# An attention pipeline one step deeper, with its PSUM banks divided by kind of product

## The chip, the cores and the metric

One NeuronCore of a Trainium2 chip runs the whole program. The metric is the device time of one execution in microseconds (us). Lower is better.

## The reference

Two transformer blocks, one after the other, on 256 image tokens and 256 context tokens of width 1024, all in float32. The first has three branches (a pooling mixer, a differential attention, a recurrent RWKV scan in both directions), a gated merge and a mixture of 32 experts. The second has two layers: an even one with a low-rank attention and a neighbourhood attention, and an odd one with a sliding-window attention with sinks, each followed by a gated feed-forward part. The change touches only the three attentions. All three compute, for blocks of 128 queries and for two heads (or two maps of one head) at a time:

```
s = q @ k.T * scale (+ bias)
p = softmax(s)                     # with a sink in the denominator in the odd layer
a = p[:, :, 0] - lam * p[:, :, 1]  # only in the differential attention
out = a @ v
```

## The kernel before

TensorE (PE in the profile), ScalarE (ACT), VectorE (DVE) and the DMA queue of SyncE (SP) each have a program of their own, written out by hand. Weights come as 1 MB tiles through a ring of six buffers (`ring`), loaded by SP in the order in which TensorE uses them. Every product of TensorE is a "job": `job(reader)` picks a PSUM bank and waits until the last reader of that bank has given it back; `done` signals the product to the engine that reads it. The kernel before picks the banks in turn, 0 to 7, whatever the product is.

The attention is cut into pairs: 128 queries, two heads or two maps. The first attention (`diff`) has 8 pairs with 512 keys, and the two maps are combined into one before the product with the values. The second (`even`) has 32 pairs, in fours of 256, 256, 512 and 512 keys: 16 of the low-rank attention, then 16 of the neighbourhood attention, of which those with 512 keys add a bias by a product with the identity. The third (`swa`) has 16 pairs with 512 keys, all with a bias and a sink.

All three engines go through the same numbered steps u. What each does in step u, in this order, is (before the change):

- TensorE (line 594): two score products of pair u, one bank for each head; the transposes of the probabilities of pair u-2, one bank for each head (one in all in `diff`), each behind a wait on `prob_` (line 624 issues the transposes); the value product of pair u-3, into one bank, behind a wait that ScalarE has copied the transposes of that pair. Score and value products are issued at line 513.
- VectorE (line 1461): the copy of the output of pair u-4 out of PSUM (line 1468); the two maxima of pair u (line 1474, and with a sink lines 1480 and 1481); the scaling of pair u-1 by the reciprocal of its sum (lines 1487, 1488 and 1496, in `diff` 1488 to 1492), which signals `prob_`.
- ScalarE (line 1194): the two exponentials of pair u (line 1204; with a sink one small one at line 1202 ahead), each with its sum; the copies of the transposes of pair u-2 to SBUF (line 1210). The bank of a score is given back when the exponential and its sum (`ACTIVATION_READ_ACCUMULATOR`) are done.

`work(u, base)` names the SBUF buffers of pair u: the probabilities `p` (three sets of two, by u % 3) and their transposes `t` (two sets, by u % 2). With five jobs in a step (four in `diff`) and eight banks in turn, a score product takes the bank of a product two steps back; in `even` and `swa` the second transpose takes the bank of the first score of the step before, and the value product that of the second.

Of the kernel before, what the change touches and what calls it, by code (L numbers as in the profile page):

```python
# [200 lines left out]
def build(nc, dram, out):  # L201
    with ExitStack() as ctx:
# [188 lines left out]
        def work(u, base):  # L391

            at = lambda o: [region(base + o + 512 * i, 512) for i in range(2)]
            return dict(p=at(1024 * (u % 3)), t=at(3072 + 1024 * (u % 2)),
                        nm=small[:, MX + 8 * (u % 4):MX + 8 * (u % 4) + 2],
                        den=small[:, MX + 8 * (u % 4) + 2:MX + 8 * (u % 4) + 4],
                        inv=small[:, MX + 8 * (u % 4) + 4:MX + 8 * (u % 4) + 6],
                        aux=small[:, MX + 8 * (u % 4) + 6:MX + 8 * (u % 4) + 8])
# [64 lines left out]
        def _(pe):  # L463
# [11 lines left out]
            def job(reader, own=False):  # L475

                b = 7 if own else st["rr"] % st["banks"]
                st["rr"] += not own
                if last_user[b] is not None:
                    who, n = last_user[b]  # L480
                    pe.wait_ge(st["back"][who], at("back_" + who, n))
                return b, reader
# [111 lines left out]
            def attention(name, pairs):  # L594
# [4 lines left out]
                for u in range(n + 3):  # L599
                    if u < n:  # L600
# [3 lines left out]
                        js = [job("act"), job("act")]  # L604
# [13 lines left out]
                    if 0 <= u - 2 < n:  # L618
                        it = pairs[u - 2]
                        for x in range(len(it["pv"])):  # L620
                            pe.wait_ge(S("prob_" + name), len(it["pv"]) * (u - 2) + x + 1)
                            j = job("act")
# [4 lines left out]
                        turned[u - 2] = gave["act"]  # L627
                    if 0 <= u - 3 < n:
                        it = pairs[u - 3]
                        pe.wait_ge(back["act"], turned[u - 3])  # L630
                        j = job("dve")
# [517 lines left out]
        def _(act):  # L1149
# [44 lines left out]
            def attention(name, pairs):  # L1194
                n = len(pairs)
                for u in range(n + 2):
# [9 lines left out]
                    if 0 <= u - 2 < n:  # L1206
                        it = pairs[u - 2]
                        for x in range(len(it["pv"])):
                            b = a.take()
                            a.given(f(it["t"][x][:, 0:it["nk"]], b[:, 0:it["nk"]], ACT.Copy))  # L1210
# [199 lines left out]
        def _(dve):  # L1410
# [50 lines left out]
            def attention(name, pairs):  # L1461

                n = len(pairs)
                for u in range(n + 4):
                    if 0 <= u - 4 < n:
                        it = pairs[u - 4]
# [620 lines left out]
```

## Time and profile before

| What | us |
|---|---|
| median of 3 runs (2712.34 to 2717.53) | 2715.67 |
| the profiled execution | 2718.1 |
| its span, from first to last instruction | 2716.3 |
| ScalarE busy in the span | 517.9 |
| VectorE busy in the span | 697.6 |
| first attention, 264.5 to 296.1 | 31.6 |
| second attention, 1666.2 to 1761.9 | 95.7 |
| third attention, 2363.7 to 2427.4 | 63.7 |

All durations and starts below are from the one profiled execution. Busy shares over the whole span say little of a change to three short stages, together 191.0 us, so the views below are cut to those stages. In a timeline row the first number is the start from the beginning of the span and the second how long the row lasts; several like instructions are merged into one row (x8). PEld is TensorE's loading of weights, which overlaps its products.

### The profile page before, as it was taken

What the parts mean: (1) busy time and instruction counts of PE and PEld (TensorE: products, weight loads), DVE (VectorE), ACT (ScalarE), POOL (GpSimd) and SP (SyncE); (2) the same over time, 40 slices, a digit from 0 to 9 for tenths busy, and PEclk for the clock granted to TensorE, in tenths of its full rate; (3) what the DMA queues carried; (4) which work ended last, traced back from release to release, by engine and by line L of the source; (5) the groups of instructions that cost most, each with busy time, mean ns of one, the idle gap of its engine ahead of it and who ended that gap; (6) DMA issues with size and microseconds to landing.
All of it is one profiled execution on the core that took longest, in us unless ns stands there. A gap on an engine that the chain in (4) does not pass through costs nothing.

```text
span 2716.3 us, 37487 instructions
## 1 busy us (share of the span) xinstructions
PE 2409.6 (89%) x15842; PEld 1466.3 (54%) x15842; DVE 697.6 (26%) x1553; ACT 517.9 (19%) x1018; POOL 0.2 (0%) x4
## 2 busy tenths in 40 slices
PE   6998749997995888888886889989999998899997
PEld 3553418886884344444443335734444443688886
DVE  2058593333113111111111105620000001251001
ACT  3111522221002111111111214611000001151001
POOL 0000000000000000000000000000000000000000
PEclk8999769998996999999998999999999999999999
DMA  8263083321330989888987120011222122203431
GB/s 326 72 245 155 6 359 114 112 102 64 139 109 22 376 364 371 370 368 363 371 371 301 47 108 1 2 62 62 77 77 78 62 77 81 78 27 130 150 130 62
DMA packets 59589, 434.06 MB, mean 160 GB/s; under 512 B 6592, under 2 KB 6848, under 8 KB 7360
## 3 DMA queue, kind: packets, MB, share of 16 engines
q1 hardware_dynamic: 57744, 420.50, 39.6%
q10 hardware_dynamic: 1712, 11.58, 1.1%
q8 instruction: 108, 1.77, 0.3%
q14 instruction: 25, 0.20, 0.0%
HBM read 431.01 MB, written 1.05 MB: 159 GB/s over the span
## 4 chain that ended last, share of the span: by engine, by line
PE 80%; DVE 8%; DMA 7%; issue 2%; ACT 2%; SPq 0%; DVEq 0%; ACTq 0%
PE bank L513 78%; DMA ring<-in_w 6%; PE bank L624 1%; ACT normed L1177 1%; DMA arena<-in_xin 1%; DVE small L1474 0%; DVE arena L1867 0%; DVE arena L1625 0%; SPq L1970 0%; PE bank L559 0%; DVE arena L1860 0%; DVE arena L1507 0%; DVE arena L1506 0%; DVE arena L1605 0%; DVE rs_t L1447 0%
## 5 line engine op out<-in xcount | busy, mean ns | idle before, releaser
L513 PE MATMUL bank<-normed,ring 128*128 128x512 f32 (+1 forms) x2688 | 877.5, 487 | 37.3 <-issue 27.5
L513 PEld LDWEIGHTS bank<-normed,ring 128*128 128x128 f32 x2688 | 514.3, 192 | 395.1 <-issue 340.2
L513 PE MATMUL bank<-arena 64*64 64x64 f32 (+6 forms) x6896 | 441.1, 251 | 53.4 <-DVE arena L1867 14.6
L513 PE MATMUL bank<-ring,arena 128*64 128x512 f32 (+1 forms) x1824 | 397.3, 611 | 49.6 <-DMA ring<-in_w 25.1
L513 PEld LDWEIGHTS bank<-arena 64*64 64x64 f32 (+4 forms) x6896 | 361.5, 146 | 140.5 <-issue 110.0
L513 PE MATMUL bank<-arena,ring 128*128 128x256 f32 (+1 forms) x1024 | 298.5, 453 | 2.8 <-DVE arena L1923 1.3
L513 PEld LDWEIGHTS bank<-ring,arena 128*64 128x64 f32 (+1 forms) x1824 | 140.5, 136 | 279.0 <-issue 249.3
L513 PEld LDWEIGHTS bank<-arena,ring 128*128 128x128 f32 x1024 | 194.2, 190 | 105.5 <-issue 84.4
L1923 DVE TENSOR_TENSOR arena<-arena,bank 128x512 f32<-128x512 f32 (+1 forms) x44 | 24.4, 554 | 431.5 <-PE bank L513 431.5
L513 PE MATMUL bank<-ring,normed 128*32 128x512 f32 (+2 forms) x576 | 115.9, 597 | 8.3 <-DMA ring<-in_w 8.3
L513 PE MATMUL bank<-arena,con 128*128 128x256 f32 (+5 forms) x304 | 92.4, 437 | 24.2 <-DVE small L1802 11.1
L1383 ACT ACTIVATE arena<-bank 128x512 f32<-128x512 f32 (+1 forms) x44 | 21.6, 490 | 410.3 <-PE bank L513 410.3
L1165 ACT ACTIVATE arena<-resid 128x512 f32<-128x512 f32 (+1 forms) x56 | 30.1, 538 | 341.4 <-DVE resid L1751 208.4
L513 PEld LDWEIGHTS bank<-arena,con 128*128 128x128 f32 (+1 forms) x304 | 52.6, 194 | 61.6 <-issue 28.8
L513 PE MATMUL bank<-arena,sw 128*64 128x128 f32 (+4 forms) x288 | 60.2, 414 | 17.9 <-DVE arena L1902 9.2
L1204 ACT ACTIVATE arena<-bank,small 128x512 f32<-128x512 f32 (+1 forms) x112 | 68.8, 619 | 36.1 <-DVE small L1474 35.2
L513 PEld LDWEIGHTS bank<-ring,normed 128*32 128x32 f32 (+1 forms) x576 | 41.4, 140 | 60.2 <-issue 45.2
L1865 DVE TENSOR_TENSOR arena<-arena,bank 128x512 f32<-128x512 f32 x17 | 11.7, 687 | 235.9 <-PE bank L513 235.9
L1474 DVE TENSOR_REDUCE small<-bank 128x1 f32<-128x512 f32 (+1 forms) x112 | 63.8, 609 | 30.7 <-PE bank L513 30.6
L1683 DVE TENSOR_TENSOR arena<-arena,bank 128x256 f32<-128x256 f32 x80 | 33.7, 421 | 100.1 <-PE bank L513 99.8
L624 PE MATMUL bank<-con,arena 128*128 128x128 f32 x352 | 49.9, 280 | 10.2 <-DVE arena L1492 6.8
L513 PE MATMUL bank<-con,arena 64*64 64x64 f32 (+2 forms) x1096 | 58.9, 223 | 0.0
(280 smaller groups left out, 1349.7 us busy)
## 6 DMA issues: line engine op xcount, KB each, us to landing
ring<-in_w SPq DMA_DIRECT2D x401, 1024.0 KB, 6.9
arena<-in_xin ACTq DMA_DIRECT2D x1, 2048.0 KB, 8.3
arena<-in_nab ACTq DMA_DIRECT2D x1, 2048.0 KB, 11.2
con<-in_con ACTq DMA_DIRECT2D x1, 1472.5 KB, 11.4
sw<-in_sw ACTq DMA_DIRECT2D x1, 1280.0 KB, 10.5
sw<-in_sw ACTq DMA_DIRECT2D x1, 1168.0 KB, 10.4
arena<-in_xin ACTq DMA_DIRECT2D x1, 1024.0 KB, 13.0
out<-arena ACTq DMA_DIRECT2D x1, 1024.0 KB, 4.0
```

Of the source, the lines that this page charges most:

```text
L513: return nc.tensor.matmul(o, l, r, start=start, stop=stop, **kw)
L624: last = nc.tensor.transpose(banks[j[0]][:, c * P:(c + 1) * P], it["p"][x][:, c * P:(c + 1) * P], ident)
L1165: a.signals(f(sq[:, k, 0:n], H[:, k, cols], ACT.Square), "squared_" + name)
L1177: ins = f(A[:, k, seg], A[:, k, seg], ACT.Identity, bias=bias, scale=sc)
L1204: a.given(f(it["p"][x][:, 0:it["nk"]], b[:, 0:it["nk"]], ACT.Exp, bias=it["nm"][:, x:x + 1], accum_out=it["den"][:, x:x + 1]))
L1383: a.given(f(sgf[:, g % 2, 0:n], b[:, 0:n], ACT.Silu))
L1474: ins = V.tensor_reduce(nm[:, x:x + 1], b[:, 0:nk], AX, MAX, negate=True)
L1683: v.gives(tt(SC[d]["Pt"], SC[d]["Pt"], j4(b, 256), ADD))
L1865: v.given(tt(actv, sgl, b[:, :], MUL))
L1923: v.given(tt(hid[:, g, 0:n], sgf[:, g % 2, 0:n], b[:, 0:n], MUL))
```

## The change

TensorE does the transposes of pair u-3 in step u, not u-2, and the value product of pair u-4, not u-3. ScalarE's copies move with the transposes, VectorE's output copy moves with the value product. The exponentials, the maxima and the scaling stay in the steps in which they were, so that one step more lies between the scaling of a pair and its transposes, and each attention has one step more in all. The probabilities have a fourth set of buffers, and the buffers of the transposes lie 1024 columns later. Inside the attentions the banks are divided: scores take 0 to 3, transposes 4 to 6, the value product bank 7, each in turn among its own.

```diff
@@ -391,7 +391,7 @@
         def work(u, base):
 
             at = lambda o: [region(base + o + 512 * i, 512) for i in range(2)]
-            return dict(p=at(1024 * (u % 3)), t=at(3072 + 1024 * (u % 2)),
+            return dict(p=at(1024 * (u % 4)), t=at(4096 + 1024 * (u % 2)),
                         nm=small[:, MX + 8 * (u % 4):MX + 8 * (u % 4) + 2],
                         den=small[:, MX + 8 * (u % 4) + 2:MX + 8 * (u % 4) + 4],
                         inv=small[:, MX + 8 * (u % 4) + 4:MX + 8 * (u % 4) + 6],
@@ -472,10 +472,14 @@
                 it, step = st["loop"]
                 return v + it * step[key]
 
-            def job(reader, own=False):
-
-                b = 7 if own else st["rr"] % st["banks"]
-                st["rr"] += not own
+            def job(reader, own=False, pool=None):
+
+                if pool:
+                    b = pool[st[pool] % len(pool)]
+                    st[pool] += 1
+                else:
+                    b = 7 if own else st["rr"] % st["banks"]
+                    st["rr"] += not own
                 if last_user[b] is not None:
                     who, n = last_user[b]
                     pe.wait_ge(st["back"][who], at("back_" + who, n))
@@ -596,12 +600,14 @@
                 n = len(pairs)
                 turned = {}
                 scored[name] = []
-                for u in range(n + 3):
+                scores, turns, values = (0, 1, 2, 3), (4, 5, 6), (7,)
+                st.update({scores: 0, turns: 0, values: 0})
+                for u in range(n + 4):
                     if u < n:
                         it = pairs[u]
                         for sem, count in it["need"]:
                             pe.wait_ge(S(sem), count)
-                        js = [job("act"), job("act")]
+                        js = [job("act", pool=scores), job("act", pool=scores)]
                         last = [None, None]
                         for c in range(0, it["nk"], SEQ):
                             for x in range(2):
@@ -615,20 +621,20 @@
                         for x in range(2):
                             done(js[x], last[x])
                         scored[name].append(([reads["act"][-2], reads["act"][-1]], gave["act"]))
-                    if 0 <= u - 2 < n:
-                        it = pairs[u - 2]
+                    if 0 <= u - 3 < n:
+                        it = pairs[u - 3]
                         for x in range(len(it["pv"])):
-                            pe.wait_ge(S("prob_" + name), len(it["pv"]) * (u - 2) + x + 1)
-                            j = job("act")
+                            pe.wait_ge(S("prob_" + name), len(it["pv"]) * (u - 3) + x + 1)
+                            j = job("act", pool=turns)
                             for c in range(it["nk"] // P):
                                 last = nc.tensor.transpose(banks[j[0]][:, c * P:(c + 1) * P],
                                                            it["p"][x][:, c * P:(c + 1) * P], ident)
                             done(j, last)
-                        turned[u - 2] = gave["act"]
-                    if 0 <= u - 3 < n:
-                        it = pairs[u - 3]
-                        pe.wait_ge(back["act"], turned[u - 3])
-                        j = job("dve")
+                        turned[u - 3] = gave["act"]
+                    if 0 <= u - 4 < n:
+                        it = pairs[u - 4]
+                        pe.wait_ge(back["act"], turned[u - 4])
+                        j = job("dve", pool=values)
                         nk = it["nk"] // P
                         rows = HALF if len(it["pv"]) == 2 else (slice(0, P),)
                         for c in range(nk):
@@ -1193,7 +1199,7 @@
 
             def attention(name, pairs):
                 n = len(pairs)
-                for u in range(n + 2):
+                for u in range(n + 3):
                     if u < n:
                         it = pairs[u]
                         for x in range(2):
@@ -1203,8 +1209,8 @@
                             b = a.take()
                             a.given(f(it["p"][x][:, 0:it["nk"]], b[:, 0:it["nk"]], ACT.Exp, bias=it["nm"][:, x:x + 1],
                                       accum_out=it["den"][:, x:x + 1]))
-                    if 0 <= u - 2 < n:
-                        it = pairs[u - 2]
+                    if 0 <= u - 3 < n:
+                        it = pairs[u - 3]
                         for x in range(len(it["pv"])):
                             b = a.take()
                             a.given(f(it["t"][x][:, 0:it["nk"]], b[:, 0:it["nk"]], ACT.Copy))
@@ -1461,9 +1467,9 @@
             def attention(name, pairs):
 
                 n = len(pairs)
-                for u in range(n + 4):
-                    if 0 <= u - 4 < n:
-                        it = pairs[u - 4]
+                for u in range(n + 5):
+                    if 0 <= u - 5 < n:
+                        it = pairs[u - 5]
                         b = v.take()
                         v.given(V.tensor_copy(it["out"], b[:, 0:P]))
                     if u < n:
```

## Rows read from the trace of the kernel before

**Rows 1.** The page, part 1: engine, busy us (share of the span), instructions

```profile
PE 2409.6 (89%) x15842; PEld 1466.3 (54%) x15842; DVE 697.6 (26%) x1553; ACT 517.9 (19%) x1018; POOL 0.2 (0%) x4
```

**Rows 2.** Windows: the three attention stages whole, then stretches inside the second and third

```profile
core 0: us, PE busy (x) PEld busy (x) DVE busy (x) ACT busy (x) POOL busy (x), PEclk, DMA share, GB/s
264.50:296.10 31.60, 24.40 (x160) 19.66 (x160) 27.73 (x59) 16.86 (x41) 0.00 (x0) 0.84 0.00 1
1666.20:1761.90 95.70, 93.92 (x800) 72.84 (x801) 65.94 (x192) 64.81 (x193) 0.00 (x0) 1.00 0.01 2
2363.70:2427.40 63.70, 59.77 (x576) 47.08 (x572) 47.15 (x144) 41.50 (x113) 0.00 (x0) 0.97 0.01 2
1681.19:1751.27 70.08, 70.08 (x605) 53.73 (x604) 49.17 (x144) 47.63 (x144) 0.00 (x0) 1.00 0.01 2
2381.01:2417.05 36.04, 36.04 (x363) 28.92 (x361) 29.30 (x91) 25.14 (x71) 0.00 (x0) 1.00 0.01 2
```

**Rows 3.** Waits in 264.5 to 296.2: who waited, total us, times, longest

```profile
DVE small L1474 <- PE bank L513: 0.8, 2, 0.4
```

**Rows 4.** Timeline, first attention: start, us, engine, operation [idle before, releaser]

```profile
292.46 0.75 DVE L1492 SCALAR_TENSOR_TENSOR arena<-arena,small 128x512 f32<-128x512 f32 x1
...
293.76 2.01 PE L513 MATMUL bank<-arena 128*128 128x128 f32 x16
...
294.86 0.29 DVE L1468 COPY arena<-bank 128x128 f32<-128x128 f32 x1 [1.44 <-PE bank L513]
295.81 0.29 DVE L1468 COPY arena<-bank 128x128 f32<-128x128 f32 x1 [0.66 <-PE bank L513]
```

**Rows 5.** Timeline, third attention, steady state

```profile
2386.21 1.29 DVE L1474 TENSOR_REDUCE small<-bank 128x1 f32<-128x512 f32 x2 [0.46 <-PE bank L513]
...
2387.20 2.16 PE L513 MATMUL bank<-arena 128*64 128x128 f32 x24
...
2389.43 1.08 ACT L1210 ACTIVATE arena<-bank 128x512 f32<-128x512 f32 x2
```

**Rows 6.** Timeline, third attention, its fill

```profile
2368.36 1.13 PE L513 MATMUL bank<-arena 64*128 64x256 f32 x8
...
2370.62 0.20 ACT L1204 ACTIVATION_READ_ACCUMULATOR arena<-bank,small 128x1 f32 x1
...
2372.05 1.28 DVE L1474 TENSOR_REDUCE small<-bank 128x1 f32<-128x512 f32 x2
...
2374.89 1.28 DVE L1474 TENSOR_REDUCE small<-bank 128x1 f32<-128x512 f32 x2
...
2376.39 2.16 PE L513 MATMUL bank<-arena 128*64 128x128 f32 x24 [0.66 <-ACT arena L1210]
```

**Rows 7.** Timeline, third attention, its last output copy

```profile
2427.06 0.29 DVE L1468 COPY arena<-bank 128x128 f32<-128x128 f32 x1 [0.58 <-PE bank L513]
```

**Rows 8.** Timeline, second attention: fill, steady state and last output copy

```profile
1669.79 0.20 ACT L1204 ACTIVATION_READ_ACCUMULATOR arena<-bank,small 128x1 f32 x1
...
1676.63 1.13 PE L513 MATMUL bank<-arena 96*128 96x256 f32 x4
...
1691.41 1.99 PE L513 MATMUL bank<-arena 96*128 96x256 f32 x8
...
1693.01 1.29 DVE L1474 TENSOR_REDUCE small<-bank 128x1 f32<-128x512 f32 x2 [1.19 <-PE bank L513]
...
1695.08 0.66 ACT L1210 ACTIVATE arena<-bank 128x256 f32<-128x256 f32 x2
...
1754.86 1.29 DVE L1474 TENSOR_REDUCE small<-bank 128x1 f32<-128x512 f32 x2 [1.38 <-PE bank L513]
...
1761.44 0.29 DVE L1468 COPY normed<-bank 128x128 f32<-128x128 f32 x1 [0.58 <-PE bank L513]
```

**Rows 9.** Windows around two idle stretches of TensorE (PEclk is the granted clock)

```profile
269.00:273.00 4.00, 0.00 (x0) 0.00 (x0) 3.89 (x9) 2.78 (x8) 0.00 (x0) 0.78 0.00 0
2370.00:2372.00 2.00, 0.34 (x4) 0.21 (x3) 1.08 (x4) 2.00 (x8) 0.00 (x0) 1.00 0.00 0
```

## The prediction

> **What bounds the kernel now.** I read the page's busy shares first, then the windows of the three attention stages, then the timelines of their beginnings, middles and ends. TensorE is busy for 2409.6 of 2716.3 us [rows 1], so only time in which TensorE waits, or a stage that another engine bounds, can be won back. The change touches three stages, 191.0 us together [rows 2]. Each has its own limit.
>
> The third attention lasts 63.7 us with TensorE busy for 59.8. From its sixth step to its last, 36.04 us, TensorE is busy for all 36.04: ten steps of 3.60 us. The second lasts 95.7 with TensorE busy for 93.9, and from 1681.19 to 1751.27 it is busy without a gap [rows 2]. In both middles the transposes never stop TensorE for their probabilities, which is the wait that the change removes. All idle time lies in the fill and in the drain: 3.9 us in the third, 1.8 in the second. The first lasts 31.6 us with VectorE busy for 27.7 [rows 2]. Once full, VectorE bounds it: its maxima waited for scores only twice, for 0.8 us in all [rows 3].
>
> So the middles stay as they are and the forecast is the sum of three fills and three drains. The most that could be won is 3.9 + 1.8 + about 1.
>
> **What stays at nothing.** The instructions are the same in number and size on every engine, and so are the DMAs. The shift of transposes and value products costs nothing in the middles, because TensorE's work per step is the same and hides ScalarE and VectorE. The new bank rule brings three waits. A score product needs the exponentials of two steps back, long done. The second transpose needs ScalarE's first copy of the step before, and the value product needs all copies of that step, as before. In the third attention the maxima start at 2386.21 and the copies of that step end at 2390.51, 4.30 later; the next value product starts at 2387.20 + 3.60 = 2390.80 [rows 5]. The slack is 0.3, and about as much for the second transpose, which stands half a microsecond ahead of each. If that cover went, behind the waiting transpose would stand the value product and the next scores, for which VectorE waits. Below nothing: if a wait on the probabilities were hidden in TensorE's issue, at most 0.1 us per step would come back in 40 steps, 4 us. I take 0, since the windows show no gap. The value product also needs the one output copy before it, made after the scaling of two pairs back, which in the middles is done over 1 us earlier.
>
> **Third attention, fill.** The third score product used free banks before and started at 2368.36. Now it takes the banks of pair 0 and waits for its exponentials, done at 2370.82 (2370.62 + 0.20) [rows 6]. ScalarE starts those late, because it loads its table first. Value product and scores with bias take 2.6 us (2387.20 to the next maxima, 2386.21 + 3.60 [rows 5]), about 1.0 and 1.6. So the maxima of pair 2 start at 2370.9 + 1.6 = 2372.5, not 2372.05; those of pair 3 follow 2.84 later (2372.05 to 2374.89 [rows 6]) at 2375.3. Only behind the exponentials of pair 3 does ScalarE copy the transposes of pair 0: it is done 4.30 later, and the first value product starts at 2379.7, not 2376.39 [rows 6]. Until then TensorE has done scores 0 to 4 and transposes 0 and 1; scores 5 start at 2380.7. Before, they start at 2376.39 + 3.60 + 1.0 = 2381.0. That is 0.3 earlier, but transposes 2 and value product 1, 3.60 - 1.6 = 2.0 us of TensorE's work, are still to do: +1.7.
>
> **Third attention, drain.** The last maxima start at 2418.3 (2386.21 + 9 x 3.60 - 0.3). The first of ScalarE's two copies of that step, of pair 12, ends 3.8 later at 2422.15, and the second transpose of pair 13 waits for its bank. From there run half a transpose (0.5), value product 12, transposes 14, value product 13 and transposes 15, 1.0 each: value product 14 starts at 2426.7. An output copy starts 1.10 after its value product (293.76 to 294.86 [rows 4]), takes 0.29, and value product 15 can only follow it, as there is one bank: 2428.1. Its output copy starts at 2429.2, against 2427.06 [rows 7]. **+2.2 for the whole stage**, in which the +1.7 is contained.
>
> **Second attention.** The same chain with halves of 256 keys. Exponentials 0 end at 1669.99, scores 2 start at 1670.04; maxima 2 follow 1.60 later (1691.41 to 1693.01), and maxima 3 about 2.0 after them (the 2.84 of above less 0.55 for the sink and 0.26 for the smaller scaling, an estimate): 1673.6. The copies of pair 0 end 2.73 later (1693.01 to 1695.08 + 0.66), value product 0 starts at 1676.4, scores 5 at 1677.0 against 1676.63 [rows 8]; undone are 1.0 of transposes and 0.55 of value product: +1.9. In the drain the last maxima start at 1754.86 + 0.35. The first copy of that step ends 2.4 later at 1757.6, then half a transpose (0.25) and the second copy, value product 28 at 1758.0, and after it 0.6 + 1.0 + 0.6 + 1.0: value product 30 at 1761.1, its copy at 1762.2, value product 31 at 1762.5, its copy at 1763.6, against 1761.44 [rows 8]. **+2.1.**
>
> **First attention.** VectorE's two waits go (-0.8), one output copy fewer stands before the last maxima (-0.2), the third scores come late at half clock (+0.3): VectorE ends its last combination at 293.21 - 0.7 (292.46 + 0.75 [rows 4]). Before, the last output copy starts 2.60 after that. Now three value products are left, one bank between them: three times (copy 0.28, hand-over 0.06, product to copy 1.10) = 4.3 [rows 4]. **+1.0.** The bounds are -1 (all of the fill kept, products overlapped) and +2.
>
> **Clock.** TensorE was idle from 269.0 to 273.0 and the granted clock, 1.00 at first, averaged 0.78, since it fell to half speed (1.2 of 2.4 GHz) on the way; around the 1.66 us gap at 2370 it stayed at 1.00 [rows 9]. The new gap in the third attention, 2368.5 to 2370.9, is 2.4 us, that in the second 1.9 us: between the two cases. If the clock falls, the next scores, 1.6 us of work on the path of maxima 2 and 3, take twice as long: +1.5 for each stage. I take one of the two; bounds 0 and +3.
>
> **Sum.** 1.0 + 2.1 + 2.2 + 1.5 = +6.8. On the profiled execution, 2718.1, that is 2724.9. The profiled execution stands 2.4 above the median of the runs, within their spread, so I add to the median: 2715.67 + 6.8 = **2722.5**. Nothing behind absorbs it: the weight ring is full during the attentions (DMA at 1 to 2 GB/s [rows 2]), and what follows starts later by as much.
>
> **A rule against this change.** In the third attention the next value product stands 3.60 us behind the one before, and its output copy, 1.10 + 0.29 after it, frees the one bank over 2 us before that [rows 4, 5]: by the rows one bank costs nothing in a middle. The Trainium skill, page "Perfetto Trace Analysis", section "Optimizing Tensor Performance", has independent products rotate through different PSUM banks, so that one is read out while the next runs, and its section "Matmul Optimizations" wants all eight in use. By it the value products, now one behind the other in bank 7, would pay for their copy in every step; that is the last rival below.
>
> **The rivals.**
> - No stage falls to half clock: +5.3, 2721.0. For it: at 2370 a gap of 1.66 did nothing. 0.20. Both fall: +8.3, 2724.0. 0.12.
> - The fills are filled: if the bank of a score came free before its exponentials end, or the first table load were not in the way, scores 2 would cover TensorE's wait as the deeper order intends. Then the fills cost nothing more and only the one-bank drains stay, about +1 to +2: 2717.2. Against it, the wait is on the last exponential. 0.15.
> - Faster: the wait for the probabilities costs TensorE time that the windows don't show. Weight loads of the transposes stand behind it; with 0.1 us in each of some 40 steps, -4.0, and the idle of the second and third fill (1.7 + 0.7) covered, minus 1.0 for the first stage: -5.4, 2710.3. It decides the case if a middle step gets shorter than 3.60. Against it: 36.04 busy in 36.04 [rows 2]. 0.06.
> - The slack of 0.3 is gone in the middle of the third attention: 0.3 in each of 11 steps, on top of +6.8: +10.1, 2725.8. 0.05.
> - Every value product of the middles pays for the copy before it: 0.29 + 0.06 in some 40 steps, 14 us on top of +6.8: 2736.5. 0.02.
>
> **How the numbers follow.** The forecast has 0.40. A measurement of this kernel can tell about 0.2%, 5.4 us, from no change. The forecast is slower by that bound, and so are two of the rivals, with a part of the 5.3 case: 0.40 less 0.08 for a short sum, 0.12, 0.05, 0.02 and 0.05 make 0.56. Faster by 0.2%: 0.05. The same: 0.39. The range has at its low end the case of filled fills, at its high end the lost slack with a median off by 1.7: 2716.5 to 2727.5.
>
> **What would show it.** In the profile after: middles of 3.60 us per step and TensorE without a gap (if shorter, the faster rival is right); the third score product of the second and third attention behind the exponentials of pair 0; the first value product 3 us later than before; a transpose in the drain that waits for ScalarE; each of the last output copies followed by a value product; a half-clock stretch at the fill of one stage. The prediction is wrong if the stages together are shorter than 191.0 us, or longer by more than 12.

## The result, and the profile after

The changed kernel takes 2725.07 us (median of 12 runs, 2720.16 to 2727.67) against 2715.74 for the kernel before (12 runs). The ratio is 1.003, 95% interval 1.0021 to 1.0039: slower, by 0.3%. The forecast was 2722.5, in a range of 2716.5 to 2727.5.

The profiled execution took 2726.51 us, with a span of 2724.7 against 2716.3. The three attentions, 8.8 us longer together, account for all of the 8.4 us between the spans. I measure each from the start of its first score product to the start of its last output copy, and split it at the start of the last maxima, so that the fill with the middle stands apart from the drain (us):

| Attention | before | after | of it fill and middle | drain |
|---|---|---|---|---|
| first | 31.25 | 32.54 | 24.03 -> 23.19 | 7.22 -> 9.35 |
| second | 95.16 | 99.44 | 88.58 -> 90.58 | 6.58 -> 8.86 |
| third | 63.86 | 67.12 | 55.44 -> 55.80 | 8.42 -> 11.32 |
| sum | 190.27 | 199.10 (+8.83) | +1.52 | +7.31 |

So most of the loss lies behind the last maxima. Part of that is work put off: in the deeper order one more pair has its transposes, and one more its value product, still to do there.

In the first attention of the changed kernel, and of the other kernels with divided banks, I count from the scores of the second pair. TensorE does those of the first pair 4.8 us earlier than before, against the work ahead of the attention:

```profile
259.91 1.13 PE L517 MATMUL bank<-arena 64*128 64x256 f32 x8 [1.34 <-DVE arena L1513]
264.80 2.08 PE L517 MATMUL bank<-arena 64*128 64x256 f32 x8 [3.76 <-DVE mod L1436]
```

It gains nothing by this, since VectorE has other work until its first maxima at 269.13. From the start that I count from to those maxima it takes 4.33 us, and 4.37 before, so the two lengths can be compared.

In the changed kernel line 513 is line 517, and every line number beyond 602 is 6 higher. These are its windows: length, then each engine's busy us, and behind POOL the granted clock PEclk. They answer to [rows 2] and [rows 9].

```profile
core 0: us, PE busy (x) PEld busy (x) DVE busy (x) ACT busy (x) POOL busy (x), PEclk, DMA share, GB/s
264.80:297.60 32.80, 23.53 (x152) 17.84 (x152) 27.57 (x59) 15.60 (x40) 0.00 (x0) 0.84 0.00 0
1667.06:1766.50 99.44, 96.00 (x800) 73.98 (x800) 66.99 (x191) 65.42 (x193) 0.00 (x0) 0.98 0.01 1
2369.18:2436.30 67.12, 62.79 (x576) 49.01 (x576) 47.02 (x143) 41.74 (x113) 0.00 (x0) 0.93 0.01 1
1682.00:1749.00 67.00, 67.00 (x574) 51.75 (x574) 47.35 (x135) 44.99 (x135) 0.00 (x0) 1.00 0.00 1
2389.94:2422.37 32.43, 32.43 (x326) 26.02 (x325) 26.35 (x82) 22.65 (x63) 0.00 (x0) 1.00 0.01 2
1672.00:1674.50 2.50, 2.50 (x7) 1.96 (x7) 1.06 (x2) 0.49 (x1) 0.00 (x0) 0.50 0.00 0
2378.00:2381.60 3.60, 3.60 (x16) 2.54 (x15) 2.66 (x9) 1.29 (x6) 0.00 (x0) 0.53 0.00 0
```

The middles (fourth and fifth row) have no gap, and the fifth holds nine steps of 3.60 us, as in [rows 2]. The last two rows show TensorE at half speed (1.2 of 2.4 GHz) at the fill of both stages. Before, neither stage fell in its fill; the third attention starts at half speed in both kernels (its first eight products take 2.08 us), rises, and only in the changed one falls again.

The timeline of TensorE in the two fills shows why. In brackets stands the idle time before a row and what ended it.

```profile
1670.90 4.30 PE L517 MATMUL bank<-arena 96*128 96x256 f32 x11 [1.88 <-ACT arena L1210]
...
2376.95 1.13 PE L517 MATMUL bank<-arena 64*128 64x256 f32 x8 [1.77 <-ACT arena L1210]
...
2384.42 0.60 PE L630 MATMUL bank<-con,arena 128*128 128x128 f32 x4
2385.78 0.63 PE L630 MATMUL bank<-con,arena 128*128 128x128 f32 x4 [0.76 <-ACT arena L1216]
```

The third score product waits for the exponentials of pair 0 (L1210), whose banks it now takes. Before, it started without a wait [rows 6]. In the third attention a transpose then waits for a copy of transposes (L1216), because there are three banks for four transposes of two steps. The second attention has the same wait, 0.67 us.

The drain of the third attention, TensorE first, then VectorE's output copies (L1474):

```profile
2427.00 0.66 PE L630 MATMUL bank<-con,arena 128*128 128x128 f32 x4
2428.94 0.63 PE L630 MATMUL bank<-con,arena 128*128 128x128 f32 x4 [1.29 <-ACT arena L1216]
2429.50 1.09 PE L517 MATMUL bank<-arena 128*64 128x128 f32 x16
...
2433.59 1.09 PE L517 MATMUL bank<-arena 128*64 128x128 f32 x16
2435.17 1.09 PE L517 MATMUL bank<-arena 128*64 128x128 f32 x16 [0.49 <-DVE arena L1474]
```

```profile
2434.73 0.29 DVE L1474 COPY arena<-bank 128x128 f32<-128x128 f32 x1 [1.76 <-PE bank L517]
2436.30 0.29 DVE L1474 COPY arena<-bank 128x128 f32<-128x128 f32 x1 [1.28 <-PE bank L517]
```

The transposes stop for 1.29 us in the middle of a pair, and the last value product waits 0.49 us for the copy of the one before it. The second attention has the same two waits, 0.37 us and 0.49 us. In the first attention the last four value products come out of one bank, and this is its loss:

```profile
292.54 0.28 DVE L1474 COPY arena<-bank 128x128 f32<-128x128 f32 x1
...
294.13 0.29 DVE L1474 COPY arena<-bank 128x128 f32<-128x128 f32 x1 [1.31 <-PE bank L517]
...
295.74 0.29 DVE L1474 COPY arena<-bank 128x128 f32<-128x128 f32 x1 [1.31 <-PE bank L517]
...
297.34 0.29 DVE L1474 COPY arena<-bank 128x128 f32<-128x128 f32 x1 [1.31 <-PE bank L517]
```

The copies stand 1.60 us apart: product to copy, copy, and back to the next product.

### The profile page after: what moved, and what is told of

Its sections match the earlier page's. It is cut to its first block, busy times and chain, and to the rows that moved or that the text cites. A ratio compares the mean times of both kernels' runs of the same rounds, so it can differ in the third digit from the quotient of the medians.

```text
span 2724.7 us, 37487 instructions
## 1 busy us (share of the span) xinstructions
PE 2413.7 (89%) x15842; PEld 1467.5 (54%) x15842; DVE 698.8 (26%) x1553; ACT 518.9 (19%) x1018; POOL 0.2 (0%) x4
## 3 DMA queue, kind: packets, MB, share of 16 engines
q8 instruction: 108, 1.77, 0.3%
## 4 chain that ended last, share of the span: by engine, by line
PE 79%; DVE 8%; DMA 7%; issue 2%; ACT 2%; SPq 0%; ACTq 0%; DVEq 0%
PE bank L517 77%; DMA ring<-in_w 7%; PE bank L630 1%; ACT normed L1183 1%; DMA arena<-in_xin 1%; DVE arena L1873 0%; DVE small L1480 0%; SPq L1976 0%; DVE arena L1631 0%; ACT arena L1210 0%; PE bank L563 0%; DVE arena L1513 0%; DVE arena L1512 0%; DVE arena L1611 0%; DVE arena L1866 0%
## 5 line engine op out<-in xcount | busy, mean ns | idle before, releaser
L1389 ACT ACTIVATE arena<-bank 128x512 f32<-128x512 f32 (+1 forms) x44 | 21.6, 490 | 410.3 <-PE bank L517 410.3
L1210 ACT ACTIVATE arena<-bank,small 128x512 f32<-128x512 f32 (+1 forms) x112 | 68.9, 620 | 43.7 <-DVE small L1480 43.6
L1191 ACT ACTIVATE arena<-bank 128x512 f32<-128x512 f32 (+1 forms) x38 | 19.3, 508 | 205.8 <-PE bank L517 205.8
```

Source lines behind the costliest of these rows:

```text
L1191: a.given(f(o, view(b, o), ACT.Copy, scale=scale))
L1210: a.given(f(it["p"][x][:, 0:it["nk"]], b[:, 0:it["nk"]], ACT.Exp, bias=it["nm"][:, x:x + 1], accum_out=it["den"][:, x:x + 1]))
L1389: a.given(f(sgf[:, g % 2, 0:n], b[:, 0:n], ACT.Silu))
```

## The experiments

The theory: the middles were full before, so the deeper order has nothing to win; it loses in fills and drains, and most of that is due to the division of the banks. The rival: depth itself is what costs. Twelve kernels were run, each compared with the kernel before in the same session (its medians: 2717.35, 2716.84, 2715.29 and 2715.79). Stage lengths below are measured as in the table above, on one profiled execution each, and a whole execution varies from the next by more than most of these differences: the ratios tell whether a whole kernel is slower, the stage lengths where.

**Depth without the division.** The changed kernel with all three pools taken out:

```diff
-                        js = [job("act", pool=scores), job("act", pool=scores)]
+                        js = [job("act"), job("act")]
...
-                            j = job("act", pool=turns)
+                            j = job("act")
...
-                        j = job("dve", pool=values)
+                        j = job("dve")
```

> The changed kernel with all eight banks in turn again; the depth stays. Stage lengths are from the first score product to the last output copy: before 31.25, 95.16 and 63.86 us, changed 32.54, 99.44 and 67.12. Theory (the order of the deeper steps costs at the fills, since the copies of pair 0 now stand behind the exponentials of pair 3; the bank split costs the gap before scores 2, the half clock that follows, and the one-bank drains): first stage 30.1, second 96.2, third 65.3, together 1.3 us longer than before, scores 2 without a gap, up to 1.7 more if the new wait for the copies of pair 0 in the third stage (3 us) brings a half clock. Rival 1 (banks alone): no stage longer than before, together 1 to 2 us shorter. Rival 2 (depth alone): as the changed kernel, 199.1.

Measured: 2720.22 us, ratio 1.0003 (0.9992 to 1.0013), which can't be told from no change. The stages are 31.04, 95.98 and 66.62, sum 193.64: +3.4 over before, where the changed kernel has +8.8. TensorE at the fill of its third attention, and a window behind it:

```profile
2374.98 1.13 PE L517 MATMUL bank<-arena 64*128 64x256 f32 x8
...
2383.33 3.64 PE L517 MATMUL bank<-arena 128*64 128x128 f32 x24 [3.10 <-ACT arena L1216]
```

```profile
2383.40:2386.80 3.40, 3.40 (x24) 2.66 (x24) 1.57 (x6) 2.52 (x7) 0.00 (x0) 0.55 0.00 0
```

The scores now run without a gap. The wait is only put off: the first value product waits 3.10 us for ScalarE's copies, which in the deeper order stand behind one more pair of exponentials, and then runs at half speed (3.64 us, not the 2.16 of [rows 5]). Depth costs mainly in the third attention, +2.76 of its +3.4, and most of that, +2.04, lies behind the last maxima. I had expected +1.3, or up to +3.0 with a half clock.

**The division without depth.** The kernel before with the bank rule of the change:

```diff
+                scores, turns, values = (0, 1, 2, 3), (4, 5, 6), (7,)
...
-                        js = [job("act"), job("act")]
+                        js = [job("act", pool=scores), job("act", pool=scores)]
...
-                            j = job("act")
+                            j = job("act", pool=turns)
...
-                        j = job("dve")
+                        j = job("dve", pool=values)
```

> The kernel before with its banks divided as in the changed one (scores 0 to 3, transposes 4 to 6, values 7); the depth is the old one. Theory: scores 2 wait for the exponentials of pair 0 (fills 0.4, 0.9 and 0.45 us longer), each drain 0.4 longer: 32.0, 96.5 and 64.7 without a half clock, and up to 1.5 more in the second and in the third stage where the granted clock falls in the gap before scores 2. Together 3 to 6 us over before. Rival 1 (banks alone): all of the 8.8 us. Rival 2 (depth alone): nothing.

Measured: 2723.12 us, ratio 1.0019 (1.0009 to 1.0030); stages 31.27, 99.43, 66.06, sum 196.76, +6.5. Its second attention:

```profile
1674.01 3.17 PE L517 MATMUL bank<-arena 96*128 96x256 f32 x8 [1.88 <-ACT arena L1210]
...
1677.83 1.99 PE L517 MATMUL bank<-arena 96*128 96x256 f32 x8
```

The same 1.88 us wait as in the changed kernel, and behind it the same eight products take 3.17 us instead of 1.99. The division alone costs about twice what depth alone does (+6.5 against +3.4) and together they cost somewhat less than the sum (+8.8). I had expected 3 to 6. Both numbers hold half-clock stretches, which no run takes out of these two kernels.

The two do not cost in the same place (us against before, split at the last maxima):

| Kernel | fill and middle | drain | sum |
|---|---|---|---|
| depth alone | -0.39 | +3.76 | +3.37 |
| division alone | +4.09 | +2.40 | +6.49 |
| both | +1.52 | +7.31 | +8.83 |

Depth starts the last maxima 0.5 and 0.6 us earlier in the first two attentions (0.7 later in the third) and puts more work behind them. The division costs most in the fill, by the wait of the third score product and the half clock behind it, and has a share in the drain.

**Two banks for the value product, two for the transposes.**

```diff
-                scores, turns, values = (0, 1, 2, 3), (4, 5, 6), (7,)
+                scores, turns, values = (0, 1, 2, 3), (4, 5), (6, 7)
```

> The changed kernel with two banks for transposes (4, 5) and two for values (6, 7) in place of three and one. Theory: the drains lose the turn of product and copy, 0.4 us per stage with two banks, up to 0.9 in the first; but the second transpose now needs both copies of the step before, and the slack worked out at 0.3 for the first copy is gone for the second: in the middle of the third stage each step becomes 3.85 to 3.9 in place of 3.60 (3 us), and about 1.5 us are lost in the last 16 pairs of the second. If the steps stay at 3.60, the slack was larger than worked out, and this is 1.2 us faster than the changed kernel.

Measured: 2725.3 us, ratio 1.0032 (1.0022 to 1.0043); 30.71, 100.09, 69.49. Against the changed kernel the first attention wins 1.8 us, its one value bank being gone, the second loses 0.7 and the third 2.4:

```profile
2385.08 0.71 PE L517 MATMUL bank<-arena,con 128*128 128x128 f32 x4
2385.96 1.11 PE L630 MATMUL bank<-con,arena 128*128 128x128 f32 x8 [0.17 <-ACT arena L1216]
...
2389.09 0.71 PE L517 MATMUL bank<-arena,con 128*128 128x128 f32 x4
...
2392.70 0.71 PE L517 MATMUL bank<-arena,con 128*128 128x128 f32 x4
2393.57 1.12 PE L630 MATMUL bank<-con,arena 128*128 128x128 f32 x8 [0.16 <-ACT arena L1216]
```

Every other step its transposes wait for ScalarE, and that step takes 4.01 us (2385.08 to 2389.09) instead of 3.61 (2389.09 to 2392.70). I had expected 3.85 to 3.9 in each; the mean is 3.81. The third bank for transposes is what kept the middle whole.

**The gap filled.** Eleven transposes of the identity into a free bank ahead of the third score product, in the second and third attention. They add work that nothing reads.

```diff
+                        if u == 2 and name != "diff":
...
+                            for _ in range(11):
+                                nc.tensor.transpose(banks[6][:, 0:P], ident, ident)
```

> The changed kernel with eleven transposes of the identity into bank 6, read by no one, in the gap before scores 2 of the second and third stage (about 1.3 us of TensorE work where it waits 1.8 to 1.9). Theory (the gap makes the granted clock fall, and scores 2 and 3 are done at half speed): the clock stays at 1.00 behind the gap; second stage 98.0 instead of 99.44, third 66.3 instead of 67.12, 2 us faster than the changed kernel. Rival (the clock costs nothing, the waits set the time): the same time within 0.3 us per stage.

Measured: 2720.91 us, ratio 1.0011 (1.0001 to 1.0022); stages 32.54, 97.95, 66.69. Windows over the two fills:

```profile
1671.60:1675.00 3.40, 3.40 (x19) 3.00 (x18) 2.57 (x7) 1.45 (x4) 0.00 (x0) 1.00 0.00 0
2374.00:2378.00 4.00, 3.57 (x27) 2.77 (x28) 3.01 (x10) 1.91 (x9) 0.00 (x0) 1.00 0.00 0
```

The clock stays at full speed, and against the changed kernel the second attention is 1.5 us shorter and the third 0.4. The third score product starts no later than without the added work (3.85 and 7.76 us into the stage, against 3.84 and 7.77), so the difference is the price of the two half-clock stretches, 1.9 us of the 8.8. The stages alone would make the whole kernel 6.9 us slower than before; its ratio says 0.3 to 6.0, so 1.9 rests on the stage lengths of one execution of each kernel.

**Transposes ahead of the scores.** Deep, banks in turn, and in each step the transposes and their copies stand before the scores and exponentials, on TensorE and on ScalarE:

```diff
                 for u in range(n + 4):
+                    if 0 <= u - 3 < n:
+                        it = pairs[u - 3]
+                        for x in range(len(it["pv"])):
+                            pe.wait_ge(S("prob_" + name), len(it["pv"]) * (u - 3) + x + 1)
+                            j = job("act")
...
                     if u < n:
                         it = pairs[u]
```

> The depth of the changed kernel with all eight banks in turn, and in each step TensorE does the transposes of pair u-3 ahead of the scores of pair u, and ScalarE the copies of them ahead of the exponentials of pair u. Theory (the deeper kernel loses at the fills and drains because the copies stand behind exponentials that they don't need): the first value product of the third stage no longer waits for the exponentials of pair 3, the drains run without a wait; stages (first score product to last output copy) 30.5, 94.8 and 61.9 us, together 3 us shorter than before (190.27); the middles stay at 3.60 us per step. Rival (depth costs by itself, one more step to fill and drain): at least as long as the deep kernel with banks in turn, 193.6.

Measured: 2715.32 us, ratio 0.9997 (0.9986 to 1.0008); stages 30.57, 95.16, 63.76. The fill and drain penalties of depth are gone, and the first attention wins 0.7. But so is most of the depth. On ScalarE the copies of pair 0 again stand between the exponentials of pairs 2 and 3, as before the change, and on TensorE its transposes between the scores of pairs 2 and 3. Only the value product and its output copy still stand one place later than before. The steps have new numbers, and what this kernel shows is that the order before, with the value product behind the next scores, costs nothing over three stages.

I had expected 3 us less than before, and got 0.8. The third middle is why. First a window over ten steps, then one step of TensorE:

```profile
2375.04:2412.59 37.55, 37.55 (x363) 29.23 (x362) 29.80 (x93) 26.53 (x76) 0.00 (x0) 1.00 0.01 2
```

```profile
2388.35 1.14 PE L517 MATMUL bank<-arena 64*128 64x256 f32 x8
2389.41 0.71 PE L517 MATMUL bank<-arena,con 128*128 128x128 f32 x4
2390.05 1.09 PE L517 MATMUL bank<-arena 128*64 128x128 f32 x16
2391.08 1.09 PE L612 MATMUL bank<-con,arena 128*128 128x128 f32 x8
2392.10 1.13 PE L517 MATMUL bank<-arena 64*128 64x256 f32 x8
```

TensorE is busy throughout and does the same products, yet a step takes 3.755 us, not 3.60. Only the order of the kinds of product differs, and with it the banks that they fall on; but the kernels before and changed differ in banks too, and both have 3.60. From the bias to the value product it takes 0.64 us here (2389.41 to 2390.05); in the old order the bias is followed by a transpose 0.55 later (2389.29 to 2389.84):

```profile
2389.29 0.71 PE L513 MATMUL bank<-arena,con 128*128 128x128 f32 x4
2389.84 1.04 PE L624 MATMUL bank<-con,arena 128*128 128x128 f32 x8
2390.80 0.44 PE L513 MATMUL bank<-arena 128*64 128x128 f32 x4
```

(These are rows of the kernel before.) The transposes run 1.02 us here until the next kind starts, and 0.96 there. These two differences, 0.09 and 0.06, make the 0.15.

**ScalarE's table ahead.** One small exponential at the head of each attention, on a constant, so that the load of the table does not wait for the first maxima. In the changed kernel it stood behind them, in the second attention here:

```profile
1668.44 1.28 ACT L1210 ACT_TABLE_LOAD   x1 [1.81 <-DVE small L1480]
```

The exponential was put into the changed kernel, the kernel before, and the kernel with transposes first:

```diff
                 n = len(pairs)
+                f(small[:, LM + 6:LM + 7], eps_c[:, 0:1], ACT.Exp)
```

> The changed kernel with one small Exp activation, on a cell that no one reads, at the start of each attention on ScalarE, so that its table is loaded before the first maximum is there. Theory: the exponentials of pair 0 end 1.2 us earlier, the gap before scores 2 shrinks from 1.8 to 0.6 us, the granted clock stays up: second stage 96.9 in place of 99.44, third 65.2 in place of 67.12. Rival (the bank wait of scores 2 costs nothing): no difference beyond 0.3.

> The kernel before with the same small activation. Theory: TensorE's waits for the first probabilities go (0.7 us in the second stage, 1.3 of 1.7 in the third): stages 31.2, 94.4 and 62.4, 2.2 us shorter than before. Rival: the time of the fills is set by VectorE, nothing changes.

> Transposes first and the small activation together. Theory: the two gains add: 30.5, 94.1 and 60.6, together 5 us shorter than before, about 0.2%. Rival: both remove the same wait, the fill of the deeper kernel hides the table load already: as transposes first alone.

Measured, in this order: 2723.09, ratio 1.0017 (1.0008 to 1.0026), stages 32.56, 96.63, 65.87; 2714.63, ratio 0.9992 (0.9983 to 1.0001), stages 31.37, 94.16, 63.32; 2713.09, ratio 0.9988 (0.9979 to 0.9997), stages 30.56, 94.25, 63.22. The changed kernel's second attention:

```profile
1670.79 3.69 PE L517 MATMUL bank<-arena 96*128 96x256 f32 x16 [0.56 <-ACT arena L1211]
```

Its wait is 0.56 us instead of 1.88, sixteen products take 3.69 us (full speed), and the stage is 2.8 us shorter. The table load was thus most of the first gap, and through the clock it cost more than its own 1.28 us. On the kernel before it brings 1.5 us over the second and third stage, where I had expected 2.2; the third fell to 63.3 and not to 62.4, and why was not looked into. With transposes first the two gains add, 0.8 and 1.4 us alone and 2.2 together, where I had expected 5.

**Back to the old order of kinds.** Banks in turn, each step transposes, value product, scores on TensorE, and copies ahead of exponentials on ScalarE. The second kernel keeps transposes, scores, value product in the first attention only, and loads the table ahead; the diff is from it.

```diff
                 for u in range(n + 4):
...
+                    for part in (score, value) if name == "diff" else (value, score):
+                        part()
```

> As transposes first (banks in turn, depth of the changed kernel), but with the scores last in each step: transposes of pair u-3, value product of pair u-4, scores of pair u. Theory (between two steps TensorE then goes from products of one shape to the next in the order of the kernel before, and it is this order alone that made a middle step of the third stage 3.75 instead of 3.60 us with transposes first): the middle step is 3.60 again, and since the sequence on TensorE and ScalarE is that of the kernel before, so is the time: stages 31.2, 95.2 and 63.9. Rival (the deeper pipeline or its banks stretch the step): 3.75 us per step stays.

> The best of the pieces: transposes, scores, values in the first stage, transposes, values, scores in the other two, banks in turn, the table ahead. Theory: 30.6 in the first stage, 94.2 and 63.3 in the others, 188.0 together against 190.3 before, 0.1% faster than before and the same as transposes first with the table ahead within its interval. Rival: the drains of the old order in the third stage cost what its middle gains.

Measured: 2720.45, ratio 1.0015 (1.0006 to 1.0025), stages 31.19, 98.28, 63.86; and 2715.94, ratio 1.0001 (0.9991 to 1.0012), stages 30.55, 97.25, 63.47. The third attention has its 3.60 us steps again, so the order of kinds made the 3.755. The second missed what I expected of it by 3.1 us in both. The first kernel's waits there (who waited, us in total, times, longest), a window, and one such place:

```profile
PE bank L612 <- DVE normed L1474: 2.3, 4, 0.6
```

```profile
1681.85:1752.00 70.15, 67.58 (x574) 51.59 (x572) 46.69 (x138) 45.28 (x138) 0.00 (x0) 1.00 0.01 2
```

```profile
1688.18 1.13 PE L517 MATMUL bank<-arena 96*128 96x256 f32 x4
...
1689.03 0.28 DVE L1474 COPY normed<-bank 128x128 f32<-128x128 f32 x1
...
1689.46 1.06 PE L612 MATMUL bank<-con,arena 128*128 128x128 f32 x8
```

The transposes (L612) wait for an output copy (L1474), since with banks in turn they take the bank of the value product two steps back. I had moved the value product ahead of the scores but left its copy in the step after, behind the maxima of those scores. Where a pair of 256 keys makes the step short, the copy comes too late: 2.57 us idle in this window.

**The copy a step earlier.** Both kernels again, with only this changed (in the second kernel, in the second and third attention only):

```diff
-                for u in range(n + 5):
-                    if 0 <= u - 5 < n:
-                        it = pairs[u - 5]
+                lag = 4
+                for u in range(n + lag):
+                    if 0 <= u - lag < n:
+                        it = pairs[u - lag]
```

> As transposes_values_scores (one step deeper, banks in turn, each step transposes, value product, scores), with one more edit: VectorE copies the output of pair u-4 in step u, not of pair u-5. What is open is why the second attention of that kernel took 98.28 us and not 95.2. My theory, from its trace: once in four steps, where a pair of 256 keys has just given short scores, the first transpose takes the bank of the value product two steps back, and VectorE copies that product one step later than it need; TensorE waits 0.3 us in the first half and 0.57 us in the second half of the stage for that copy, eight times, 3.1 to 3.5 us in all. With the copy a step earlier the waits go: stages 31.2, 95.2 and 63.9, sum 190.3, as before; ratio 1.000, median within 1 us of before. Rival A: the waits come from the order of the product shapes or from the scaling of the probabilities and stay: second stage still about 98.3, ratio 1.0015. Rival B: the earlier copy makes VectorE wait for the value product ahead of the maxima and costs as much as it gives: second stage 96 to 98, and the first, where VectorE is the bound, over 31.5.

> As order_by_stage_table_ahead (first attention transposes, scores, value product; second and third transposes, value product, scores; ScalarE's exponential table loaded ahead), with the output copy of pair u-4 in step u in the second and third attention; the first keeps pair u-5. Same theory: the second stage falls from 97.25 to 94.2, the others stay at 30.55 and 63.4: sum 188.2, 2.1 less than before, ratio 0.9990, median about 2713.5. Rival A: second stage stays 97.25, ratio 1.0001. Rival B: second 95 to 97, ratio 0.9995.

Measured: 2714.43, ratio 0.9997 (0.9988 to 1.0007), stages 31.60, 95.16, 63.86; and 2711.44, ratio 0.9984 (0.9975 to 0.9993), stages 30.60, 94.16, 63.36. The first kernel's window over the same middle:

```profile
1675.00:1746.00 71.00, 71.00 (x618) 54.73 (x616) 49.46 (x145) 48.47 (x146) 0.00 (x0) 1.00 0.01 1
```

No idle time is left, and the second attention fell by 3.12 us in one kernel and 3.09 in the other: the late copy was all of the miss.

But look at what the first kernel has become. Its scores stand last in the step and have the number of the next, so TensorE does scores 2, transposes 0, scores 3, transposes 1, value product 0, scores 4, which is the order of the kernel before; ScalarE and VectorE have their old orders too. The trace agrees: second and third attention are as long as before to the hundredth (95.16 and 63.86), and every timeline row of ScalarE and VectorE in them starts within 0.03 us of its old place, counted from the start of the stage. The first value product of the third starts 13.19 us in, as it did before:

```profile
2359.22 2.08 PE L517 MATMUL bank<-arena 64*128 64x256 f32 x8 [9.48 <-DVEq L456]
...
2372.41 2.16 PE L517 MATMUL bank<-arena 128*64 128x128 f32 x24 [0.66 <-ACT arena L1207]
```

It is no deeper than the kernel before. The first kernel of the last section was therefore the kernel before with its output copies one step late, and 3.1 us is what that lateness cost. The first attention is 0.35 us longer here (31.60 against 31.25) in the same order; what makes that is open, and smaller differences there should not be read. The second kernel beats both the kernel before and the changed one, and not by depth: its second and third attention are those of the kernel before with the table ahead (94.16 and 63.36 against 94.16 and 63.32), its first has the value product behind the next scores (30.60 against 31.25). Its stages are 2.15 us shorter than before, 0.0008 of the whole; the ratio's interval holds that, and the rest of its 0.0016 no run here explains.

## Why the prediction was right, and where its sizes were off

**What bounds the kernel, and the middles at nothing: right.** Both middles kept TensorE without a gap and steps of 3.60 us. The faster rival needed a wait on the probabilities hidden in the middles, and falls with this. The slack of 0.3 us held, so the rival of the lost slack falls too; the kernel with two transpose banks, in which it broke, shows how near it was. The last rival (every value product pays for the copy before it) is refuted in the two middles that TensorE bounds: one bank cost nothing there. In the first attention the value product does wait for the copy before it, 0.19 us at 285.25, and VectorE hides it. What it says is true in the drains, where value products follow each other closely: 0.49 us at the end of two stages, and turns of 1.60 us in the first.

**The sum.** Each term against its measurement, the clock taken out by the kernel with the filled gap (97.95 and 66.69):

| Term | predicted | measured |
|---|---|---|
| first attention | +1.0 | +1.29 |
| second, without the clock | +2.1 | +2.79 |
| third, without the clock | +2.2 | +2.83 |
| half clock | +1.5 | +1.92 |
| sum | +6.8 | +8.83 |

*First attention.* The fill and middle won 0.84 about as worked out (0.8 + 0.2 - 0.3 = 0.7); VectorE waited 0.34 us for the third scores, as I had it. The drain was mis-sized: I took a turn of product, copy and hand-over as 1.44 us (4.3 for three), and it is 1.60, which is 0.5 more over three turns. The hand-over from the copy to the next product is 0.15 us (292.82 to 292.97), not 0.06, and from the product to its copy it is 1.16 (292.97 to 294.13), not 1.10.

*Second and third.* The third score product waited for the exponentials of pair 0, and the first value product of the third attention started at 2386.34, 17.2 us into the stage, against 13.2 before: 4.0 later, of it 0.4 by the clock (with the gap filled it starts 16.7 into the stage), where I had 3.3. By the last maxima nearly all of that is made up, as predicted: without the clock fill and middle are +0.50 and -0.07, predicted +0.35 and -0.3. The drains were mis-sized again: +2.28 and +2.90, where the working gives +1.8 and +2.5. I put the last turn at 1.4 us, with no hand-over in it; it is 1.57. In the third attention the rest is ahead of value product 12, which starts 4.5 us after the last maxima (2424.98 to 2429.50), not 4.35.

*Clock.* This is the step that failed in its choice. I let one of two stages fall, from two cases: a gap of 4 us with a fall, one of 1.66 without. Both fell, after waits of 1.88 and 1.77 us, so the rival "both fall" (+8.3, 2724.0), to which I gave 0.12, came true and is nearest to the result. Its number is nearest partly by luck: it has 3.0 for the clock, which cost 1.9, and 5.3 for the rest, which cost 6.9. The price was not twice 1.5: the second attention paid 1.5, but the third only 0.4, because there TensorE, once faster, waits for ScalarE soon after. With the gap filled it reaches the transposes of pair 0 1.6 us sooner (11.08 us into the stage, against 12.66), and then stops twice (in this kernel L1216 are the exponentials and L1222 the copies of the transposes):

```profile
2379.49 1.13 PE L517 MATMUL bank<-arena 64*128 64x256 f32 x8 [0.70 <-ACT arena L1216]
...
2382.83 0.63 PE L636 MATMUL bank<-con,arena 128*128 128x128 f32 x4 [1.13 <-ACT arena L1222]
```

The first wait, of scores 4 for the exponentials of pair 2, the changed kernel does not have; the second is 0.76 us there. So 1.1 of the 1.6 us are waited away again. In the second attention only 0.2 us are (0.86 against 0.67).

**Which part of the change costs.** The prediction did not split this. Depth alone makes +3.4 us and the division of the banks alone +6.5; taking the division out of the changed kernel wins 5.5, taking the depth out 2.3. The rival theory, that depth itself is what costs, falls as the main cause, though half of the drain's loss comes with depth alone (3.76 of 7.31). No run here shows depth at no cost. Where its cost is gone (189.49 against 190.27 before), the copies and the transposes are back at their old places, and only the value product is later.

## What to carry to other kernels

Depth can win in a middle only where some engine waits there. Here the bounding engine was busy for all of it, and depth lengthened the drains. So first read the middle, then count what each end pays. Banks in turn lend a fill and a drain all eight; the division by kind took that away just there, though it cost nothing in the steady state. Write down the order of instructions on each engine without the step numbers: the last kernels here were taken for deeper ones, and in most of their attentions they had the order before under new numbers, at first with a copy too late. And when an order is turned round on one engine, follow every hand-back of a buffer: the value product moved ahead needed its copy moved ahead on VectorE too, and that was worth 3.1 us.

## What the runs showed of the hardware

The order of kinds of product alone changed TensorE's pace: the same products take 3.60 us in the order scores, bias, transposes, values and 3.755 us in the order scores, bias, values, transposes, with no idle time in either; both kernels with the second order have it. The bias is followed 0.09 us sooner by a transpose than by a value product, and the transposes 0.06 us sooner by a value product than by a score. What in the engine does this was not looked into.

A short wait can cost beyond itself: 1.88 us of idle time at the second attention's fill brought 1.5 us more by the half clock behind it. The Trainium skill, page "Perfetto Trace Analysis", section "Matmul Optimizations", says that the engine scales its power by use, so that products should come back to back; the kernel with the gap filled agrees, with clock 1.00 and 1.5 us less.
